# Moving the activations to 2048-byte boundaries, and loading the residual stream in two parts

## The chip, the core and the metric

The kernel runs on one core of a Trainium2 chip, as one program. The metric is the device time of an execution in microseconds (us), and the number that counts is the median of the runs. Five engines work on their own instruction streams and meet at semaphores: PE (TensorE, the matmuls), DVE (VectorE), ACT (ScalarE), POOL (GpSimd) and SP (SyncE, which here only issues DMAs). Data lives in SBUF (128 partitions, one flat byte address within each) and in PSUM, into which PE writes.

## The reference, cut to what matters

The input is one sequence of 512 tokens with 1024 features in float32. A state-space layer (S5) with a gated output and an MLP come first, then a layer of sliding-window attention and another MLP, then a last norm:

```python
h = x
h = h + s5_mixer(rmsnorm(h, norm_mix[0]), ...)          # 64 groups of 16 channels, 64 states each
#   inside: y = gelu(S5(u) + d * u);  z = y @ w_glu + b_glu;  return val * sigmoid(gate)
h = h + square(relu(rmsnorm(h, norm_mlp[0]) @ w_mlp_in[0])) @ w_mlp_out[0]
k, v = split(rmsnorm(h, norm_kv) @ w_kv + b_kv)
h = h + attention(rmsnorm(h, norm_mix[1]), k, v, sinks)  # window 128
h = h + square(relu(rmsnorm(h, norm_mlp[1]) @ w_mlp_in[1])) @ w_mlp_out[1]
return rmsnorm(h, norm_final)
```

## The kernel before, in words

**Layout.** Activations are held feature by token: a tile is 128 features by 512 tokens, 2048 bytes in each partition, and eight tiles make the 1024 features. `h` is the residual stream (8 tiles). `hid` and `act` hold operands of matmuls as pairs of float32r tensors, a high part (`[:, 0]`) and a low part (`[:, 1]`), so that three matmuls (high by high, high by low, low by high) give nearly float32 accuracy.

**Weight units.** Every dense layer is cut into units: one unit is a panel of 128 output features by all 1024 inputs (4096 bytes in each partition, 512 KB), 24 matmuls of 128 by 128 by 512. There are 164 units in a fixed order, numbered from the gated output of S5 (0 to 15: `U_GLU`) through the first MLP, K/V, Q, O and the second MLP. SP loads panel `u` into one of two buffers (`raw`), POOL splits it into `w_hi` and `w_lo` (the function `split`, which copies at L405 and subtracts at L408, in four slots), and PE multiplies (`unit`, L1114 to L1116; or `paired`, L1078 to L1080, which runs two units tile by tile). The semaphores between them are `raw_in` (a panel has landed), `w_split` (units split so far) and `unit_done` (units multiplied so far). PE waits at a unit's start for `w_split`; the first `paired` call takes units 0 and 1, the second (`paired(U_GLU + 2, ...)`) units 2 and 3. For K and V the operands change sides for one part (L1176 to L1178): there `act` is the stationary operand and the weights are what streams.

**Before the units.** S5 runs in eight steps of 8 groups ("octets"). PE's matmuls there are small and in plain float32; ACT evacuates their results, POOL and DVE do the complex arithmetic, and for each octet SP issues eight small DMAs (L298) that lay a small table `k_even` or `k_odd` out as a block Toeplitz matrix, `toep`. `y_mm` counts the octets that PE has finished. Units 0 and 1 are run in pieces between the last octets' work.

**SP's queue.** SP issues in program order: first the parameters, the input `xy`, the columns `col` and panels 0 and 1; then the 64 Toeplitz DMAs; then all of `h` (L305), panels 2 and 3 (L308), panels 4 to 7 (L311), the attention mask, and a loop over the rest. It cannot load `h` earlier in this version, because `w_2`, one of three buffers of S5 weights (octets 2 and 5), lies on the first 4608 bytes of `h`. ACT and DVE wait for `h` (`s_h`) before the gated output's epilogue (L531, L829, L833).

**Where things lie.** The tensors are allocated one behind the other, so each address follows from the sizes ahead of it. `h` starts at byte 16512 of a partition (8 x 2048 + 128), `w_hi` at 41088 and `w_lo` at 57472 (both 128 bytes above a multiple of 2048), and `hid` at 89184, which is 43 x 2048 + 1120; `act` and `qT`, which share one place behind it, are at 154720, again 1120 above a multiple.

Of the kernel before, what the change touches and what calls it, by code (L numbers as in the profile page):

```python
# [14 lines left out]
P = 128  # L15
D = 1024
L = 512
KT = D // P
# [66 lines left out]
SETUP_EXP, SETUP_PH, SETUP_L, SETUP_X, SETUP_MS = 4, 10, 23, 43, 47  # L85
SETUP_R8, SETUP_RSTD = 6, 10
T_DMA = 16 * J

STAT_A = (1, 3, 4, 5)

# [5 lines left out]
def build(nc, panels, xu_d, x_d, lam_d, prm_d, dd_d, cst_d, mask_d, col_d, out_d):  # L96
    ctx = ExitStack()
    with ctx:
        def sb(name, shape, dt=F32, where=ctx):
            return where.enter_context(nc.sbuf_tensor(name, shape, dt))  # L100

        def sem(name):
            return ctx.enter_context(nc.semaphore(name))


        before = ExitStack()
        w_2 = sb("w_2", [P, 2, OGP, J + 1, C], where=before)
        before.close()
        h = sb("h", [P, KT, L])
# [20 lines left out]
        t1 = sb("t1", [P, L])  # L130
        t2 = sb("t2", [P, 2, L])
        gate_sb = sb("gate_sb", [P, 2])
        phases = t1.rearrange("p (g k) -> p g k", k=NK)
        ph_round = rstd.rearrange("p (g k) -> p g k", k=NK)

# [71 lines left out]
        s_lam, s_prm, s_cst, s_h, s_col, s_mask, s_dd = (sem(n) for n in (  # L207
            "lam_in", "prm_in", "cst_in", "h_in", "col_in", "mask_in", "dd_in"))
# [31 lines left out]
        def wait(eng, s, value):  # L240

            if not (isinstance(value, int) and value <= 0):
                eng.wait_ge(s, value)
# [33 lines left out]
        @block.sync  # L277
        def _(sp):
            sp.dma_start(lam[:], lam_d).then_inc(s_lam, 16)
            sp.dma_start(prm[:], prm_d).then_inc(s_prm, 16)  # L280
            sp.dma_start(cst[:], cst_d).then_inc(s_cst, 16)
            sp.dma_start(dd[:], dd_d).then_inc(s_dd, 16)
            for c in range(4):
                part = slice(2 * c * OCT, (2 * c + 2) * OCT)
                sp.dma_start(xy[:, part, :], xu_d[:, part, :]).then_inc(s_xu[c], 16)
            sp.dma_start(col[:], col_d).then_inc(s_col, 16)
            for s in range(2):
                sp.dma_start(raw[:, s, :], panels[s]).then_inc(raw_in[s], 16)

            def toeplitz(o):  # L290

                q = o % 2
                wait(sp, k_evac, 4 * o + 4)
                wait(sp, zeroed, 3)
                wait(sp, y_mm, o - 1)
                for j in range(J):
                    r = J - 1 - j
                    sp.dma_start(toep[r * C:(r + 1) * C, q, :, :, j * C:],  # L298
                                 k_out[q][:, :, :, 0:(J - j) * C]).then_inc(t_in[q], 16)

            for o in range(NO):
                toeplitz(o)

            wait(sp, y_mm, NO - 2)
            sp.dma_start(h[:], x_d).then_inc(s_h, 16)  # L305
            for u in (2, 3):
                wait(sp, w_split, u - 1)
                sp.dma_start(raw[:, u % 2, :], panels[u]).then_inc(raw_in[u % 2], 16)  # L308
            for u in range(4, 8):
                wait(sp, w_split, u - 1)  # L310
                sp.dma_start(raw[:, u % 2, :], panels[u]).then_inc(raw_in[u % 2], 16)  # L311
            wait(sp, y_lo, KT)
            sp.dma_start(mask[:], mask_d).then_inc(s_mask, 16)
            with sp.Fori(4, NU // 2) as i:
                for s in range(2):
                    sp.wait_ge(w_split, 2 * i + s - 1)
                    sp.sem_inc(passed, 1)
                    sp.dma_start(raw[:, s, :], panels[2 * i + s]).then_inc(raw_in[s], 16)
            for m in range(KT):
                wait(sp, out_t, m + 1)  # L320
                sp.dma_start(out_d[m], h[:, m, :]).then_inc(out_s, 16)
            sp.wait_ge(out_s, 16 * KT)
# [100 lines left out]
        def _(a):  # L423
# [51 lines left out]
            def evacuate_k(o):  # L475
                wait(a, k_mm, o + 1)
                wait(a, t_in[o % 2], T_DMA * (o // 2))
                for x in range(4):
# [44 lines left out]
                wait(a, stat_v, 2 * n + 2)  # L523
                act_fn(rstd[:], stat[:], ACT.Sqrt).then_inc(stat_a, 1)

            wait(a, s_h, 16)
            wait(a, s_col, 16)
            with a.Fori(0, KT // 2) as i:
                for e in range(2):
# [69 lines left out]
        def _(v):  # L599
# [164 lines left out]
            def y_to_lo(o):  # L764
                wait(v, y_hi, o + 1)
                if o == NO - 2:
                    wait(v, t_in[1], T_DMA * NO // 2)
                tt(hid[:, 0, 1, o, :], ps[:, 7, :], hid[:, 0, 0, o, :].bitcast(F32), sub).then_inc(y_lo, 1)
# [50 lines left out]
                    nc.vector.reciprocal(scol[:], scol[:]).then_inc(stat_c, 1)  # L819


            wait(v, s_h, 16)
            wait(v, s_col, 16)
            with v.Fori(0, KT // 2) as i:
                for e in range(2):
# [162 lines left out]
        def _(pe):  # L988
# [51 lines left out]
            def outputs(o):  # L1040

                q = o % 2
                wait(pe, gelu_done, o)
                wait(pe, t_in[q], T_DMA * (o // 2 + 1))
                for g in range(OGP):
# [350 lines left out]
```

## Time and profile before

| | us |
|---|---|
| three runs | 1140.38, 1139.22, 1138.17 |
| median | 1139.22 |
| the profiled execution, its own time | 1139.55 |
| its span (first to last instruction) | 1137.7 |
| PE busy in the span | 1084.1 (95%) |
| PEld (weight loads, beside PE) busy | 879.7 (77%) |
| DVE, POOL, ACT busy | 640.1, 718.9, 202.7 |
| mean clock granted to PE | 0.98 of full |

PE is the engine that sets the time: it is busy in 95% of the span, and in the two MLPs in all of it. A matmul's record overlaps the next one's, so the rate of the matmuls is read from the distance between their starts, not from their durations. Idle time on the other engines costs nothing until PE waits for them.

### The profile page before, as it was taken

What the parts mean: (1) busy time and instruction counts of PE and PEld (TensorE: products, weight loads), DVE (VectorE), ACT (ScalarE), POOL (GpSimd) and SP (SyncE); (2) the same over time, 40 slices, a digit from 0 to 9 for tenths busy, and PEclk for the clock granted to TensorE, in tenths of its full rate; (3) what the DMA queues carried; (4) which work ended last, traced back from release to release, by engine and by line L of the source; (5) the groups of instructions that cost most, each with busy time, mean ns of one, the idle gap of its engine ahead of it and who ended that gap; (6) DMA issues with size and microseconds to landing.
All of it is one profiled execution on the core that took longest, in us unless ns stands there. A gap on an engine that the chain in (4) does not pass through costs nothing.

```text
span 1137.7 us, 16116 instructions
## 1 busy us (share of the span) xinstructions
PE 1084.1 (95%) x5720; PEld 879.7 (77%) x5720; DVE 640.1 (56%) x766; ACT 202.7 (18%) x439; POOL 718.9 (63%) x563
## 2 busy tenths in 40 slices
PE   4889999999999999999999999969999999999995
PEld 1778788788888888888788888757888888888884
DVE  7996574776316316417837876586762263164164
ACT  4763111111001001001105445111110010010000
POOL 7995977587667666667753220486766676676650
PEclk9799999999999999999999999989999999999998
DMA  4224332232222222222221110132223222222211
GB/s 184 33 33 134 130 111 92 74 111 92 93 92 93 92 93 93 99 98 89 90 81 62 38 38 1 38 111 66 101 92 98 93 99 99 93 92 93 92 56 74
DMA packets 34720, 97.91 MB, mean 86 GB/s; under 512 B 11120, under 2 KB 11504, under 8 KB 34416
## 3 DMA queue, kind: packets, MB, share of 16 engines
q1 hardware_dynamic: 34672, 97.24, 25.9%
q8 instruction: 34, 0.56, 0.2%
q14 instruction: 14, 0.11, 0.0%
HBM read 92.77 MB, written 2.10 MB: 83 GB/s over the span
## 4 chain that ended last, share of the span: by engine, by line
PE 84%; issue 4%; DVE 4%; ACT 3%; POOL 2%; DMA 2%; SPq 1%; DVEq 1%; ACTq 0%; POOLq 0%
PE ps L1114 23%; PE ps L1116 23%; PE ps L1115 23%; PE ps L1230 3%; PE ps L1207 2%; PE ps L1078 2%; PE ps L1079 2%; PE ps L1080 2%; PE ps L1219 1%; DVE act L803 1%; SPq L298 1%; DMA raw<-panels_in 1%; PE ps L1054 1%; PE ps L1016 1%; PE ps L1032 1%
## 5 line engine op out<-in xcount | busy, mean ns | idle before, releaser
L408 POOL TENSOR_TENSOR w_lo<-raw,w_hi 128x1024 fp32r<-128x1024 f32 x164 | 421.6, 2571 | 13.7
L1114 PE MATMUL ps<-hid,w_hi 128*128 128x512 f32 x736 | 294.7, 400 | 2.8 <-issue 1.9
L1116 PE MATMUL ps<-hid,w_lo 128*128 128x512 f32 x736 | 291.7, 396 | 0.0
L1115 PE MATMUL ps<-hid,w_hi 128*128 128x512 f32 x736 | 291.7, 396 | 0.0
L332 POOL TENSOR_TENSOR gate_sb<-gate_sb 128x1 f32<-128x1 f32 x164 | 42.5, 259 | 363.1 <-PE ps L1116 314.5
L1114 PE MATMUL ps<-act,w_hi 128*128 128x512 f32 x464 | 183.7, 396 | 1.2 <-DVE act L803 1.2
L1116 PE MATMUL ps<-act,w_lo 128*128 128x512 f32 x464 | 183.5, 396 | 0.0
L1115 PE MATMUL ps<-act,w_hi 128*128 128x512 f32 x464 | 183.5, 395 | 0.0
L405 POOL TENSOR_SCALAR w_hi<-raw 128x1024 fp32r<-128x1024 f32 x164 | 180.4, 1100 | 0.0
L862 DVE TENSOR_TENSOR h<-ps,h 128x512 f32 x64 | 44.2, 690 | 236.7 <-PE ps L1116 236.7
L1114 PEld LDWEIGHTS ps<-hid,w_hi 128*128 128x128 f32 x736 | 138.6, 188 | 36.9 <-issue 2.0
L1116 PEld LDWEIGHTS ps<-hid,w_lo 128*128 128x128 f32 x736 | 138.7, 188 | 33.6
L1115 PEld LDWEIGHTS ps<-hid,w_hi 128*128 128x128 f32 x736 | 138.7, 188 | 33.1
L851 DVE TENSOR_TENSOR hid<-t,hid 128x512 fp32r<-128x512 f32 x64 | 129.3, 2020 | 44.9 <-ACT hid L543 44.9
L543 ACT ACTIVATE hid<-t 128x512 fp32r<-128x512 f32 x64 | 40.7, 635 | 470.1 <-DVE t L849 470.1
L1114 PEld LDWEIGHTS ps<-act,w_hi 128*128 128x128 f32 x464 | 87.2, 188 | 22.6 <-DVE act L803 1.6
L1116 PEld LDWEIGHTS ps<-act,w_lo 128*128 128x128 f32 x464 | 87.2, 188 | 21.1
L1115 PEld LDWEIGHTS ps<-act,w_hi 128*128 128x128 f32 x464 | 87.2, 188 | 21.0
L847 DVE SCALAR_TENSOR_TENSOR t<-ps,rstd 128x512 f32<-128x512 f32 x64 | 44.2, 690 | 64.3 <-PE ps L1116 64.0
L849 DVE TENSOR_TENSOR t<-t 128x512 f32<-128x512 f32 x64 | 67.2, 1050 | 2.2
L800 DVE TENSOR_TENSOR acc<-acc,t 128x512 f32<-128x512 f32 x32 | 66.0, 2062 | 3.2
L517 ACT ACTIVATE act<-h,col x24 | 17.4, 725 | 143.2 <-DVEq L864 79.6
(209 smaller groups left out, 1084.3 us busy)
## 6 DMA issues: line engine op xcount, KB each, us to landing
raw<-panels_in SPq DMA_DIRECT2D x164, 512.0 KB, 3.2
xy<-xu_in SPq DMA_DIRECT2D x4, 512.0 KB, 7.8
h<-x_rows_in SPq DMA_DIRECT2D x1, 2048.0 KB, 9.0
out<-h SPq DMA_DIRECT2D x8, 256.0 KB, 2.1
prm<-prm_in SPq DMA_DIRECT2D x1, 1280.0 KB, 5.6
mask<-mask_in SPq DMA_DIRECT2D x1, 512.0 KB, 4.1
dd<-dd_in SPq DMA_DIRECT2D x1, 256.0 KB, 5.9
toep<-k_even SPq DMA_DIRECT2D x4, 64.0 KB, 2.3
```

Source lines behind the costliest of these rows:

```text
L332: nc.gpsimd.tensor_tensor(gate_sb[:, 0:1], gate_sb[:, 1:2], gate_sb[:, 1:2], ALU.mult)
L405: nc.gpsimd.tensor_scalar(w_hi[:, s, :], raw[:, s % 2, :], 1.0, 0.0, ALU.mult, ALU.add).then_inc(w_hi_done, 1)
L408: nc.gpsimd.tensor_tensor(w_lo[:, s, :], raw[:, s % 2, :], w_hi[:, s, :].bitcast(F32), ALU.subtract).then_inc(w_split, 1)
L543: act_fn(hid[:, par, 0, m, :], t2[:, m % 2, :], ACT.Copy).then_inc(hid_hi, 1)
L800: tt(acc[:], acc[:], t1[:], ALU.add).then_inc(sq_acc, 1)
L847: stt(t1[:], ps[:, m % 4, :], 0.0, rstd[:], ALU.max, ALU.mult).then_inc(bank_free, 1)
L849: tt(t2[:, m % 2, :], t1[:], t1[:], ALU.mult).then_inc(hid_sq, 1)
L851: tt(hid[:, par, 1, m, :], t2[:, m % 2, :], hid[:, par, 0, m, :].bitcast(F32), ALU.subtract).then_inc(hid_lo, 1)
L862: tt(tile(h, m), ps[:, s, :], tile(h, m), ALU.add).then_inc(bank_free, 1)
L1114: mm(ps[:, bank, :], w_hi[:, s, w], x[:, 0, k, :], start=(k == 0), stop=False)
L1115: mm(ps[:, bank, :], w_hi[:, s, w], x[:, 1, k, :], start=False, stop=False)
L1116: last = mm(ps[:, bank, :], w_lo[:, s, w], x[:, 0, k, :], start=False, stop=(k == KT - 1))
```

## The change

It has two parts. (1) Behind `gate_sb` a tensor of 232 float32 (928 bytes) that nobody uses is allocated, so that everything behind it lies 928 bytes higher: `hid` at 90112, which is 44 x 2048, and `act` at 155648, which is 76 x 2048. The S5 tensors and the Toeplitz tables move by the same 928 bytes; `h`, `raw`, `w_hi` and `w_lo` stay. (2) `h` is loaded by two DMAs. The first takes tiles 0 to 4 and is issued at the program's start behind panels 0 and 1; the second takes tiles 5 to 7 and is issued behind panels 2 and 3. `w_2` moves onto tiles 5 to 7 of `h`, clear of the first part. ACT and DVE wait for both parts.

```diff
@@ -85,6 +85,8 @@
+H_FIRST = KT - 3
+TO_LINE = 232
@@ -104,6 +106,7 @@
         before = ExitStack()
+        sb("h_first", [P, H_FIRST, L], where=before)
         w_2 = sb("w_2", [P, 2, OGP, J + 1, C], where=before)
         before.close()
         h = sb("h", [P, KT, L])
@@ -130,6 +133,7 @@
         gate_sb = sb("gate_sb", [P, 2])
+        sb("to_line", [P, TO_LINE])
@@ -286,6 +290,7 @@
             for s in range(2):
                 sp.dma_start(raw[:, s, :], panels[s]).then_inc(raw_in[s], 16)
+            sp.dma_start(h[:, 0:H_FIRST, :], x_d[:, 0:H_FIRST, :]).then_inc(s_h, 16)
@@ -302,10 +307,10 @@
             wait(sp, y_mm, NO - 2)
-            sp.dma_start(h[:], x_d).then_inc(s_h, 16)
             for u in (2, 3):
                 wait(sp, w_split, u - 1)
                 sp.dma_start(raw[:, u % 2, :], panels[u]).then_inc(raw_in[u % 2], 16)
+            sp.dma_start(h[:, H_FIRST:, :], x_d[:, H_FIRST:, :]).then_inc(s_h, 16)
             for u in range(4, 8):
@@ -523,7 +528,7 @@
-            wait(a, s_h, 16)
+            wait(a, s_h, 32)
@@ -819,7 +824,7 @@
-            wait(v, s_h, 16)
+            wait(v, s_h, 32)
```

The instruction streams of PE, DVE, ACT and POOL hold the same operations in the same order as before; only SP's changes. This is SP's stream before, from its last Toeplitz DMA of the last octet (`k_odd` is the table, `x_rows_in` the residual stream in memory, `panels_in` the weights; sizes are partitions by elements):

```order
L298 DMA toep<-k_odd 16x8x16
L305 DMA h<-x_rows_in 128x4096
L308 DMA raw<-panels_in 128x1024 x2
L311 DMA raw<-panels_in 128x1024 x4
L313 DMA mask<-mask_in 128x1024
```

And this is the same place after; panels 2 and 3 are now next to the Toeplitz DMA, and three eighths of `h` come behind them:

```order
L303 DMA toep<-k_odd 16x8x16
L312 DMA raw<-panels_in 128x1024 x2
L313 DMA h<-x_rows_in 128x1536
L316 DMA raw<-panels_in 128x1024 x4
L318 DMA mask<-mask_in 128x1024
```

The other five eighths are issued at the program's start. SP's first rows before:

```order
1 L279 DMA lam<-lam_in 128x233
2 L280 DMA prm<-prm_in 128x2560
3 L281 DMA cst<-cst_in 128x384
4 L282 DMA dd<-dd_in 128x512
5 L285 DMA xy<-xu_in 128x1024 x4
6 L286 DMA col<-col_in 128x346
7 L288 DMA raw<-panels_in 128x1024 x2
8 L298 DMA toep<-k_even 16x1024
```

And after, where one DMA stands between panels 0 and 1 and the first Toeplitz DMA:

```order
5 L289 DMA xy<-xu_in 128x1024 x4
6 L290 DMA col<-col_in 128x346
7 L292 DMA raw<-panels_in 128x1024 x2
8 L293 DMA h<-x_rows_in 128x2560
9 L303 DMA toep<-k_even 16x1024
```

So the whole of `h` moves in two pieces: 2560 elements of each partition ahead of S5, 1536 behind it.

## Rows read from the trace of the kernel before

**Rows 1.** Busy time of each engine, from the page.
```profile
PE 1084.1 (95%) x5720; PEld 879.7 (77%) x5720; DVE 640.1 (56%) x766; ACT 202.7 (18%) x439; POOL 718.9 (63%) x563
```

**Rows 2.** PE's waits: line waited for, us in total, times, longest.
```profile
PE ps L1078 <- DVE h L967: 9.4, 1, 9.4
PE ps L1078 <- POOL w_lo L408: 2.7, 1, 2.7
PE ps L1047 <- DMA toep<-k_even: 1.2, 1, 1.2
```

**Rows 3.** PE's timeline: start us, us, instruction [idle before <-releaser].
```profile
115.15 0.40 PE L1080 MATMUL ps<-hid,w_lo 128*128 128x512 f32 x1
118.21 0.50 PE L1078 MATMUL ps<-hid,w_hi 128*128 128x512 f32 x1 [2.65 <-POOL w_lo L408]
118.54 0.39 PE L1079 MATMUL ps<-hid,w_hi 128*128 128x512 f32 x1
...
196.47 0.40 PE L1116 MATMUL ps<-hid,w_lo 128*128 128x512 f32 x1
196.71 0.40 PE L1078 MATMUL ps<-act,w_hi 128*128 128x512 f32 x1
```

**Rows 4.** POOL's timeline, splits of units 2 to 5.
```profile
110.89 0.19 POOL L332 TENSOR_TENSOR gate_sb<-gate_sb 128x1 f32<-128x1 f32 x1 [13.55 <-DMA raw<-panels_in]
...
115.81 2.34 POOL L408 TENSOR_TENSOR w_lo<-raw,w_hi 128x1024 fp32r<-128x1024 f32 x1
118.11 0.19 POOL L332 TENSOR_TENSOR gate_sb<-gate_sb 128x1 f32<-128x1 f32 x1
...
124.96 2.70 POOL L408 TENSOR_TENSOR w_lo<-raw,w_hi 128x1024 fp32r<-128x1024 f32 x1
```

**Rows 5.** SP's timeline, DMA issues between 90 and 120 us.
```profile
94.91 5.50 SPq L298 DMA_DIRECT2D toep<-k_odd  x8
100.45 0.59 SPq L305 DMA_DIRECT2D h<-x_rows_in  x1
101.08 0.91 SPq L308 DMA_DIRECT2D raw<-panels_in  x2
114.60 13.42 SPq L311 DMA_DIRECT2D raw<-panels_in  x4
```

**Rows 6.** The page's DMA issues: KB each, median us from issue to landing.
```profile
raw<-panels_in SPq DMA_DIRECT2D x164, 512.0 KB, 3.2
h<-x_rows_in SPq DMA_DIRECT2D x1, 2048.0 KB, 9.0
```

**Rows 7.** Issue to landing at L308 (panels 2 and 3), then L288 (panels 0 and 1).
```profile
DMA to landing us min/median/max: 9.6/10.0/10.4
...
DMA to landing us min/median/max: 9.9/10.3/10.7
```

**Rows 8.** SP's timeline at the start: panels 0 and 1, first Toeplitz issues.
```profile
5.21 0.96 SPq L288 DMA_DIRECT2D raw<-panels_in  x2
33.56 5.98 SPq L298 DMA_DIRECT2D toep<-k_even  x8
```

**Rows 9.** DVE's timeline: last S5 state of L762, then the first epilogue.
```profile
101.87 0.41 DVE L762 TENSOR_TENSOR st<-ps,rs 128x256 f32<-128x256 f32 x1
117.81 0.75 DVE L829 SCALAR_TENSOR_TENSOR t<-ps,col,t 128x512 f32<-128x512 f32 x1 [3.98 <-ACT t L531]
118.71 1.72 DVE L833 TENSOR_TENSOR h<-t,h 128x512 f32 x1 [0.16 <-DVE t L829]
```

**Rows 10.** PE's timeline in the first MLP, matmuls 24 apart.
```profile
305.12 0.40 PE L1116 MATMUL ps<-hid,w_lo 128*128 128x512 f32 x1
...
310.72 0.40 PE L1116 MATMUL ps<-hid,w_lo 128*128 128x512 f32 x1
```

**Rows 11.** PE's timeline in K/V: the first, two in the middle, the last of 96.
```profile
570.35 0.28 PE L1176 MATMUL ps<-w_hi,act 128*128 128x256 f32 x1
...
571.40 0.28 PE L1176 MATMUL ps<-w_hi,act 128*128 128x256 f32 x1
...
571.75 0.28 PE L1176 MATMUL ps<-w_hi,act 128*128 128x256 f32 x1
...
581.43 0.27 PE L1178 MATMUL ps<-w_hi,act 128*128 128x256 f32 x1
```

**Rows 12.** PE's timeline, two matmuls behind its long wait.
```profile
763.12 0.63 PE L1079 MATMUL ps<-act,w_hi 128*128 128x512 f32 x1
763.55 0.63 PE L1080 MATMUL ps<-act,w_lo 128*128 128x512 f32 x1
```

**Rows 13.** Windows: us, busy of PE, PEld, DVE, ACT, POOL, PEclk, DMA share, GB/s.
```profile
100.00:200.00 100.00, 97.34 (x506) 77.71 (x505) 52.27 (x44) 17.52 (x22) 72.15 (x54) 1.00 0.36 127
760.00:765.00 5.00, 3.75 (x9) 2.97 (x10) 4.66 (x5) 2.01 (x2) 4.25 (x2) 0.50 0.35 105
1000.00:1100.00 100.00, 100.00 (x431) 80.49 (x430) 44.36 (x38) 4.45 (x7) 67.40 (x53) 1.00 0.27 92
```

**Rows 14.** The page's groups of matmuls in `unit`: count, busy, mean ns.
```profile
L1114 PE MATMUL ps<-hid,w_hi 128*128 128x512 f32 x736 | 294.7, 400 | 2.8 <-issue 1.9
L1114 PE MATMUL ps<-act,w_hi 128*128 128x512 f32 x464 | 183.7, 396 | 1.2 <-DVE act L803 1.2
```

## The prediction

> **What bounds the kernel now.** I began with the page's first part: PE is busy in 95% of the span [rows 1], so only what makes PE wait or changes its pace can move the end. Two questions follow: where does PE stand still, and at what pace does it run. The list of PE's waits answers the first. The reader should look there for waits that this change can reach: one, 2.7 us at L1078 on POOL's split (the second `paired` call, units 2 and 3) [rows 2]. The long one, 9.4 us on DVE at L967, is in front of the second MLP, and neither part of the change touches what leads to it. In the timeline the last matmul of units 0 and 1 starts at 115.15 us and the first of unit 2 at 118.21 [rows 3]. The window from 100 to 200 us has PE busy for 97.34 of 100 us [rows 13]: this wait is the whole loss there.
>
> Then I followed the wait back. POOL stood idle for 13.55 us until panel 2 landed, began at 110.89, and ended the second split at 115.81 + 2.34 = 118.15 us, which is what PE waited for [rows 4]. Panel 2 was issued at 101.08 [rows 5] and took 9.6 us to land, panel 3 took 10.4 [rows 7]; the median panel takes 3.2 us [rows 6]. The reason stands in the row ahead of it: the 2048 KB of `h` were issued at 100.45 [rows 5] and took 9.0 us [rows 6], so they landed at 109.5, then panel 2 at 110.7, and panel 3 (issued some 0.5 us behind it) at 111.9. They land in the order of issue, 1.2 us apart, as if in one queue: 512 KB in 1.2 us is the rate.
>
> **Part 2, the two loads of `h`.** *Removed:* the copy of 2048 KB in front of panels 2 and 3. The first of them takes its place at 100.45 us. The copy of `h` there needed 9.0 us, of which 4 x 1.2 = 4.8 us is transfer by the rate above, and 4.2 us is start-up (the last Toeplitz DMAs are still draining). Panel 2 then lands at 100.45 + 4.2 + 1.2 = 105.9 us at the latest, and with the median 3.2 us at 103.7 at the earliest. POOL is ready: besides the panel its third split waits only for octet 7's states, which DVE ends at 101.87 + 0.41 = 102.3 us [rows 9]. From panel 2's landing to the end of both splits it took 118.15 - 110.7 = 7.45 us. So the splits end between 111.1 and 113.3 us, and PE wants them at 115.38 (one matmul behind 115.15). The wait goes, with 2.1 us to spare in the worse case.
>
> *What it is worth.* From 115.15 to 118.21 are 3.06 us [rows 3]; without a wait a step takes 0.23 to 0.24 us, as where PE goes from one unit to the next at 196.47 and 196.71 [rows 3]. That is 2.82 us. The first matmul behind the wait is also slow to start the next one (0.33 us from 118.21 to 118.54, against 0.23), another 0.10. Sum: 2.9 us.
>
> *What is late next.* The second part of `h` (3/8 of it, 1.8 us of transfer) lands 1.2 + 1.8 us behind panel 2, at 106.7 to 108.9 us, and nobody needs it before L829 and L833 at 117.81 and 118.71 us [rows 9]; these follow PE's end of units 0 and 1, which does not move, so ACT and DVE wait for nothing new. Panel 4 was issued when POOL had split unit 2, at 114.60 [rows 5], and will be issued some 5 us earlier. Units 4 and 5 are wanted by PE from 115.38 + 2 x 5.6 = 126.6 us on (a unit is 5.60 us [rows 10]). Their splits need unit 1 and then unit 2 of PE: in the trace they took from 118.11 to 127.66 us [rows 4], 9.55 us for two with a wait of half a microsecond in between. Begun at 115.4 they end at 125.0; unit 4's is done by 120. The cover is 6 us for unit 4 and 7 for unit 5 (wanted at 132.2), and grows, since POOL needs about 4.5 us for a unit and PE 5.6. From there on PE's later waits are for DVE work that itself follows PE's last unit, so they move along with it; I count no part of the 2.9 us as given back.
>
> *Added:* one DMA of 5 of 8 tiles at the start. Panels 0 and 1 are issued from 5.21 to 6.17 us and land up to 10.7 us after [rows 7, 8], by 16.4. The new copy is behind them: 2.5 panels, 3.1 us, done by 19.5. The next DMA that SP issues is the Toeplitz one at 33.56 us [rows 8]. Cost nothing, covered by 14 us; SP's issue of 0.5 us falls into the same gap. If the queue did not serve in order but shared, the parameters would be up to 3.1 us late and the gain would be gone; the landings 1.2 us apart speak for order.
>
> **Part 1, the 928 bytes.** No operation is added; the question is whether an address changes a pace. PE's pace is the costly one: 3 x (736 + 464) matmuls of 512 columns in `unit` [rows 14] and 3 x 96 more in `paired` are 3888, so one nanosecond in each is 3.9 us. The row: 24 of them take 310.72 - 305.12 = 5.60 us, 233.3 ns each, at a granted clock of 1.00 (2.4 GHz) [rows 10, 13]. That is 560 cycles for 512 columns. At a clock of 0.50 (1.2 GHz) they start 0.43 us apart [rows 12, 13], 512 cycles: at the lower clock the 48 extra cycles are not there, so at the higher one something that feeds PE limits it. 20 ns x 3888 = 78 us is thus the most that an address could give back.
>
> Does it come from the address? K/V is the test that lies in the trace, for there the streamed operand is the weights, at 128 and not 1120 bytes above a multiple of 2048. 95 steps take 581.43 - 570.35 = 11.08 us [rows 11], 116.6 ns for 256 columns: 280 cycles, the same 35/32 per column. And its operand moves by 512 bytes with each k, so it runs over a multiple of 2048 only at k = 3 and k = 7; the three matmuls of k = 3 take 571.75 - 571.40 = 0.35 us, the same as the average of 3 x 116.6 = 0.35. So crossing a 2048-byte boundary costs nothing that is visible, and the offset of 1120 costs no more than that of 128. I take zero. Ends for the range: nothing excludes boundaries of 512 bytes or less. If each 512-byte boundary cost 12 of the 48 cycles (4 in an operand of 2048 bytes, 2 in K/V's two pieces of 512, which fits both rows), an aligned operand would have 3 inside instead of 4: 5 ns x 3888 = 19 us less. With 256-byte boundaries, 6 cycles each, it is 2.5 ns and 10 us less. On the other side the same 10 us more, if aligned operands met one boundary more.
>
> For the Toeplitz DMAs and S5's tensors, moved by the same 928 bytes, the bound is what PE waits for them: 1.2 us once [rows 2], a gain at most; a landing slower by as much would cost the same. Nearest to zero, which I take.
>
> The Trainium skill (page "TensorE: Matmul & The Clock Gate", section "Wait — 56ns, not 53.3ns?") has back-to-back matmuls at N / 2.4 GHz plus about 2.5 ns, 215.7 ns for 512 columns; this trace disagrees with 233.3 ns for float32r. By that rule 17.5 ns x 3888 = 68 us would be there to be won, if the address were what is in the way; the page doesn't say that it is. Against it stands a second rule: the page "SBUF — State Buffer" (section "Door 1: The DMA port swizzle", its note on cachelines) has lines of 16 bytes, and the old address 89184 is a multiple of 16 already, so by this rule the sum stays at 2.9 us.
>
> **The sum.** The profiled execution: 1139.55 - 2.9 = 1136.65 us. It was 0.33 above the median of 1139.22, so for a median I say **1136.4 us**, 0.25% less. A measurement of this kernel tells about 0.2% (2.3 us, below 1136.9) from no change, so the forecast lies just beyond it.
>
> **The rivals.**
> (a) *PE's pace rises.* One cause behind the 48 cycles (boundaries of 512 bytes or less) makes it 19 or 10 us less beside the 2.9: 1117 or 1127 us; the whole of it would be 1136.4 - 78 = 1058. For it: the extra cycles are real and feed-bound. Against it: K/V's same ratio at another offset, and no dependence on k. 10% together.
> (b) *The gain is given back.* The 2.9 us come back as a wait later: either the early copy delays the parameters (3.1 us), or PE's clock falls for longer somewhere, since behind its 9.4 us wait it is at 0.50 [rows 2, 13] and a shift of 3 us may lengthen that stretch. 1138.5 to 1139.5 us. 16%.
> (c) *Slower.* At the new address a streamed operand of 2048 bytes costs one stop more than it does now, in all 3888 matmuls; it decides from 1.3 ns each on ((2.9 + 2.3) / 3888). With the 2.5 ns of above: 1136.4 + 9.7 = 1146 us. For it only that one nanosecond is so dear; against it the same K/V rows. 5%.
> (d) *The change doesn't do what it says*: panels 2 and 3 stay late since what delays them is the start-up of 4.2 us and not `h`. Even twice that start-up ends the splits at 117.55 instead of 118.15, 0.6 us won: 1138.6. The landings 1.2 us behind `h` speak against it. 3%.
>
> **How the numbers follow.** Forecast 66%, (a) 10, (b) 16, (c) 5, (d) 3. The forecast's own spread is the 1.2 us of the Toeplitz term and about 1 us by which runs differ (1138.17 to 1140.38): 1135.0 to 1137.6. The range of 8 in 10 takes in (b) and (d) and leaves out (a) and (c): 1134.6 to 1139.8. Faster: four fifths of the forecast's 66% lie beyond 0.2%, with (a) 0.63; within 0.2%: the rest of it, (b) and (d), 0.32; slower 0.05.
>
> **What would show it.** Step by step in the profile after: no wait of the second `paired` call on POOL's split, and 0.23 us between the starts where now are 3.06; panel 2 landing between 103.7 and 105.9 us and POOL's idle before it down to 6 to 8 us; both parts of `h` landed by 19.5 and 109; the first Toeplitz issue still near 33.6. PE's 24 matmuls in 5.60 us and K/V's 96 in 11.1 as before: any other number there makes part 1 real and my forecast wrong, the more so as one nanosecond is 3.9 us. A new wait of PE behind 118 us, or a longer stretch at a clock of 0.50, would be rival (b).

## The result, and the profile after

The changed kernel took 1133.03 us in the median (five runs, 1132.36 to 1134.47) against 1139.22: the ratio is 0.9947, with a 95% interval of 0.9933 to 0.9962. That is 6.2 us less. The forecast was 1136.4 with a range from 1134.6 to 1139.8: the direction was right, and the gain more than twice what was forecast (6.2 us against 2.8). The profiled execution took 1132.71 us, its span 1130.9.

The page's first part answers to [rows 1]. PE is busy 7.3 us less, with the same 5720 matmuls:

```profile
PE 1076.8 (95%) x5720; PEld 878.0 (78%) x5720; DVE 637.5 (56%) x766; ACT 202.4 (18%) x439; POOL 719.6 (64%) x563
```

PE's waits answer to [rows 2] (line waited for, us in total, times, longest). The wait of the second `paired` call for POOL's split is gone; the long one is still there, and the one for the first Toeplitz DMAs (L1052 now) has grown by 2.0. It costs nothing: PE's work ahead of it was done earlier (more of it at full clock), while the DMAs landed when they did before, and PE goes on at 40.81 us (40.83 before):

```profile
PE ps L1083 <- DVE h L972: 9.5, 1, 9.5
...
PE ps L1052 <- DMA toep<-k_even: 3.2, 1, 3.2
```

PE's timeline where units 0 and 1 end answers to [rows 3]: the next matmul starts 0.23 us behind the last.

```profile
114.47 0.39 PE L1085 MATMUL ps<-hid,w_lo 128*128 128x512 f32 x1
114.70 0.40 PE L1083 MATMUL ps<-hid,w_hi 128*128 128x512 f32 x1
```

POOL's timeline answers to [rows 4]. Its idle time ahead of the split of unit 2 has fallen from 13.55 to 6.35 us, and both splits end at 110.9, 3.8 us ahead of PE:

```profile
103.62 0.19 POOL L337 TENSOR_TENSOR gate_sb<-gate_sb 128x1 f32<-128x1 f32 x1 [6.35 <-DMA raw<-panels_in]
...
108.51 2.39 POOL L413 TENSOR_TENSOR w_lo<-raw,w_hi 128x1024 fp32r<-128x1024 f32 x1
```

SP's timeline answers to [rows 5] and [rows 8]: the early part of `h` at 6.34 us, the first Toeplitz DMA at 33.87 (33.56 before), then panels 2 and 3 and the late part.

```profile
6.34 0.49 SPq L293 DMA_DIRECT2D h<-x_rows_in  x1
33.87 5.69 SPq L303 DMA_DIRECT2D toep<-k_even  x8
...
99.63 1.00 SPq L312 DMA_DIRECT2D raw<-panels_in  x2
100.67 0.43 SPq L313 DMA_DIRECT2D h<-x_rows_in  x1
```

Their time from issue to landing, for L312 (panels), L293 (early part) and L313 (late part); the first answers to [rows 7]:

```profile
DMA to landing us min/median/max: 3.8/4.2/4.5
...
DMA to landing us min/median/max: 13.0/13.0/13.0
...
DMA to landing us min/median/max: 7.2/7.2/7.2
```

So panel 2 landed at 103.4 us, `h` at 19.3 and 107.9. All of that is as predicted, but for 0.3 us at panel 2. (One size was off without effect: the late part of `h` landed 3.3 us behind panel 3, where the prediction counted 1.8 us for it.) What was not predicted stands in PE's timeline in the first MLP, which answers to [rows 10]: the two matmuls 24 apart are 5.57 us apart and not 5.60.

```profile
299.74 0.39 PE L1121 MATMUL ps<-hid,w_lo 128*128 128x512 f32 x1
...
305.31 0.39 PE L1121 MATMUL ps<-hid,w_lo 128*128 128x512 f32 x1
```

Over longer stretches 24 matmuls take 5.600 us in the gated output and 5.577 in both MLPs. K/V went the other way; its first and last matmul (see [rows 11]) give 11.39 us for 95 steps, 119.9 ns each instead of 116.6:

```profile
565.38 0.28 PE L1181 MATMUL ps<-w_hi,act 128*128 128x256 f32 x1
...
576.77 0.29 PE L1183 MATMUL ps<-w_hi,act 128*128 128x256 f32 x1
```

This table sets the two profiled executions side by side. Each entry is a start in PE's timeline; the last column is what each stretch contributed.

| PE's start of | before | after | shift so far | contributed |
|---|---|---|---|---|
| last matmul of units 0, 1 | 115.15 | 114.47 | -0.68 | S5 and PE's clock in it: -0.7 |
| first of unit 2 | 118.21 | 114.70 | -3.51 | the wait: -2.8 |
| first of MLP 0 | 196.71 | 193.10 | -3.61 | -0.1 |
| last of MLP 0 | 555.72 | 550.70 | -5.02 | the pace: -1.4 |
| first of Q | 583.57 | 578.92 | -4.65 | K/V's pace and a longer wait ahead of it: +0.4 |
| last of O | 751.49 | 744.96 | -6.53 | PE's clock behind K/V: -1.6; the rest: -0.3 |
| last of MLP 1 | 1122.11 | 1114.48 | -7.63 | the pace: -1.4; wait and half clock ahead of it: +0.3 |
| end of the span | 1137.74 | 1130.93 | -6.81 | PE's clock in the tail: +0.8 |

The clock term can be seen in windows (us, busy of PE, PEld, DVE, ACT, POOL, granted clock, DMA share, GB/s). This one is of the kernel before, just behind its K/V wait: 10 matmuls at 0.50, which is 1.2 GHz.

```profile
584.20:587.60 3.40, 3.40 (x10) 2.62 (x9) 0.51 (x1) 0.00 (x0) 3.32 (x4) 0.50 0.27 93
```

And this one of the changed kernel at the same place: 16 matmuls at 1.00, 2.4 GHz.

```profile
579.20:582.60 3.40, 3.40 (x16) 2.76 (x15) 0.86 (x1) 0.00 (x0) 3.32 (x4) 1.00 0.16 35
```

### The profile page after: what moved, and what is told of

Read it like the earlier page. It is cut to its first block, busy times and chain, and to the rows that moved or that the text cites. A ratio compares the mean times of both kernels' runs of the same rounds, so it can differ in the third digit from the quotient of the medians.

```text
span 1130.9 us, 16118 instructions
## 1 busy us (share of the span) xinstructions
PE 1076.8 (95%) x5720; PEld 878.0 (78%) x5720; DVE 637.5 (56%) x766; ACT 202.4 (18%) x439; POOL 719.6 (64%) x563
## 4 chain that ended last, share of the span: by engine, by line
PE 83%; DVE 8%; issue 5%; ACT 2%; POOL 1%; DVEq 1%; DMA 0%; ACTq 0%; SPq 0%
PE ps L1119 23%; PE ps L1120 23%; PE ps L1121 23%; PE ps L1235 3%; PE ps L1083 2%; PE ps L1085 2%; PE ps L1084 2%; PE ps L1212 2%; PE ps L1224 1%; DVE act L808 1%; DVE h L867 1%; ACT s_sb L578 1%; ACT hid L522 1%; DVE t L802 0%; DMA prm<-prm_in 0%
## 5 line engine op out<-in xcount | busy, mean ns | idle before, releaser
L413 POOL TENSOR_TENSOR w_lo<-raw,w_hi 128x1024 fp32r<-128x1024 f32 x164 | 420.5, 2564 | 13.7
```

The costliest lines, as they stand in the source:

```text
L413: nc.gpsimd.tensor_tensor(w_lo[:, s, :], raw[:, s % 2, :], w_hi[:, s, :].bitcast(F32), ALU.subtract).then_inc(w_split, 1)
```

## The experiments

A time given without a number of runs is that of a single run. S5 takes unequal time from run to run: over all the profiles PE's last matmul of units 0 and 1 starts between 114.3 us (`before_again`) and 118.3 us (`dist_0`), after 7 to 27 us at half clock in S5. So a single run proves little by its total time; its paces, read from the trace, are what counts.

"Distance" below is the address of `hid` less that of `w_hi`, modulo 256 bytes; that of `act` and of `w_lo` is the same. It is 224 in the kernel before and 128 in the changed one.

**Each part alone, and both kernels again.** `split_only` is the changed kernel without the 928 bytes, `shift_only` the kernel before with them.

```diff
-        sb("to_line", [P, TO_LINE])          # split_only, against the changed kernel
+        sb("to_line", [P, 232])              # shift_only, against the kernel before
```

> Part 2 alone: h in two loads, hid still 1120 bytes above a multiple of 2048. Theory A (the two parts act apart: the loads remove PE's wait at units 2 and 3, the addresses set PE's pace): about 2.9 us under before, near 1136.3; 24 matmuls take 5.600 us everywhere as in before, K/V 116.7 ns a step. Theory B (the pace came by chance or with the time at which PE begins, not with the address): the pace of the first MLP drops to about 5.578 us for 24 here too, and the time is near 1133.5.

Measured: 1134.28 us median (8 runs), ratio 0.9963 (0.9951 to 0.9976); 5.600 us for 24 and 116.7 ns in K/V everywhere. The pace did not come with the loads, but the time is 2 us lower than theory A had it: 5.3 us under the kernel before beside it by the medians, 4.2 by the ratio. In its profile PE is at full clock behind K/V:

```profile
577.00:583.00 6.00, 4.14 (x24) 3.42 (x23) 2.57 (x5) 0.00 (x0) 4.63 (x5) 1.00 0.00 0
```

> Part 1 alone: 928 bytes, h in one load. Theory A: PE's wait of 2.7 us at units 2 and 3 is back, 24 matmuls in the two MLPs take 5.577 us, K/V 120 ns a step, and the time is some 2.5 us under before (3888 matmuls, of which those of the MLPs, 3072, gain 0.95 ns: 2.9, less 0.3 in K/V), near 1136.6. Theory B: the pace is 5.600 us for 24 and the time that of before.

Measured: 1136.69 us (11 runs), ratio 0.9975 (0.9966 to 0.9984), with the wait for POOL back (2.3 us idle, 2.7 from one start to the next), 5.577 us for 24 and 119.9 ns in K/V: near theory A's 1136.6. In this profile the half clock came behind the wait for unit 2, at 119.1 us, and not behind K/V:

```profile
119.10:122.50 3.40, 3.40 (x8) 2.75 (x9) 3.21 (x3) 0.72 (x1) 3.32 (x3) 0.50 0.45 154
```

> The changed kernel a second time. If PE's pace follows from the addresses, the same pattern returns: 5.600 us for 24 in the gated output, 5.577 in both MLPs, 120 ns in K/V. If it depends on the moment at which the stream begins, the stretches can take other values, for instance 5.600 in an MLP. The 3.4 us at half clock behind K/V (in the profile of before at 584 us, not in that of after) may come or not.

Measured: 1136.01 us. 24 matmuls took 5.577 us in the gated output and 5.600 in both MLPs, the reverse of the first profile, K/V 118.7 ns, and the half clock came behind K/V, at 580.7 us. So the same program at the same addresses runs at either of two paces. The slower one is not the kernel before's: its steps alternate between 229 and 238 ns, those of the kernel before between 232 and 235.

> The kernel before a second time. Address: 5.600 us for 24 matmuls in every stretch, 116.7 ns in K/V. Moment: some stretch at 5.577. The half clock at 584 us for 3.4 us comes again if it follows from the kernel's own activity, and may be missing if it is chance; without it the time is some 1.2 us less.

Measured: 1138.39 us, 5.600 us for 24 in every stretch, K/V 116.7, the half clock at 583.4 us again.

**The clock behind the waits.** The added matmuls are these; `before_fill` has both places, `split_fill` (on `split_only`) the second alone:

```diff
+            def fill(n):
+                for _ in range(n):
+                    mm(ps[:, 7, 0:256], ident, cst[:, 0:256], start=True, stop=True)
+            wait(pe, y_lo, KT)
+            fill(6)
             paired(U_GLU + 2, 2, hid[:, 0], (y_lo, 1))
...
+            wait(pe, bank_free, 4 + U_KV + 2)
+            fill(4)
             query_unit(0, range(KT))
```

> The kernel before (h in one load, old addresses) with matmuls added that nobody reads, where PE waits: 6 of 0.43 us in front of units 2 and 3 and 4 behind K/V, so that PE is busy there. Theory A (the 2 us by which splitting the loads won more than the wait itself are stretches of 3.4 us at half clock that follow from the waits at units 2/3 and behind K/V; each costs 1.5 to 1.7 us): the half clock behind units 1 and behind K/V is gone, and the time falls by 1.3 to 1.7 us under before, to about 1138.0, with a narrow spread. Rival B (the clock has nothing to do with it): the time stays at 1139.5 and single runs spread as before.

Measured: 1137.49 us median of 12 runs, 2.0 under the 1139.51 of the kernel before beside it; but four of the twelve are above 1138.9, and the ratio of 0.999 (0.9981 to 0.9998) says 1.1 us. In the profile both places are at full clock; behind unit 1:

```profile
117.40:120.80 3.40, 3.40 (x16) 2.72 (x16) 3.21 (x3) 0.71 (x1) 3.14 (x3) 1.00 0.42 154
```

> h in two loads at the old addresses, with the 4 added matmuls behind K/V. Theory A: the half clock behind K/V can no longer come, the time is that of the two-load kernel in its usual runs (1134.2) or up to 0.5 above it, since the added matmuls can end a little late, and about 3 us under before_fill, which is the wait of 2.8 us alone. Rival B: the difference to before_fill stays at 5 us.

Measured: 1134.69 us (1134.19 to 1135.05), 2.8 us under `before_fill`: with the clock held up, the two loads are worth about what the wait was, as predicted (by the two ratios it is 3.4 us, with some 2 us of uncertainty). It is 0.4 us above `split_only`, so in the kernel with two loads the added matmuls won nothing. Theory A holds, though the size of the clock's share is known only as 1 to 2 us.

**Whose address sets the pace.** `all_shift` puts the 928 bytes in front of `h`, so that weights and activations move together; `both_at_0` puts 1920 bytes there and 1056 behind `gate_sb`.

```diff
+        sb("pad", [P, 232])                  # all_shift, no to_line;  both_at_0: 480, TO_LINE = 264
         before = ExitStack()
```

> 928 bytes put in front of h instead of behind gate_sb, h in two loads: hid and act are on multiples of 2048 as in the changed kernel, and the weights move along (w_hi and w_lo from 128 to 1056 above a multiple), so that the distance between the two operands is that of before. If the streamed operand's own address sets the pace: steps alternate by 229 and 238 ns or run in the seven-step pattern, 5.577 or 5.600 us for 24, and K/V takes 118.6 to 119.9 ns. If the distance between the two operands that PE reads at once sets it: steps of 232 and 235, 5.600 everywhere, K/V 116.7.

Measured: 1134.27 us, and exactly the numbers of the kernel before: steps of 232 and 235 ns, 5.600 us for 24, K/V 116.7. `hid` is on a multiple of 2048 here, and nothing is won by it. Two matmuls 24 apart:

```profile
300.26 0.40 PE L1120 MATMUL ps<-hid,w_lo 128*128 128x512 f32 x1
...
305.86 0.40 PE L1120 MATMUL ps<-hid,w_lo 128*128 128x512 f32 x1
```

The distance counts, not `hid`'s own address.

> h, raw, w_hi, w_lo, hid and act all on multiples of 2048 (the weights now too), h in two loads. Own address: as in the changed kernel, 5.577 or 5.600, K/V 118.6 to 119.9. Distance between the operands: a value not seen yet, since the distance is new (0); if both reads want the same line at once it could be slower than 5.600.

Measured: 1118.56 us. The guess that it might be slower was wrong by a wide margin: 24 matmuls take 5.440 us, 226.7 ns each.

**The distance, step by step.** Only `TO_LINE` differs from the changed kernel:

```diff
-TO_LINE = 232
+TO_LINE = 264      # dist_0;   392: dist_512;   328: dist_256;   280: dist_64;   320: dist_224
```

> The changed kernel with 1056 unused bytes in place of 928: hid and act 128 bytes above a multiple of 2048, as w_hi and w_lo are, so that the distance between the two operands that PE reads at once is 0 modulo 2048, while neither is on a multiple. Distance theory: the pace of both_at_0, 5.440 us for 24 matmuls, K/V 120 ns, and a time near 1119. Own-address theory (a multiple of 2048 of each operand is what counts): 5.577 to 5.600, as in the kernel before or the changed one, near 1133 to 1136.

Measured: 1117.39 us median of 5, ratio 0.9798 (0.978 to 0.9817), 5.440 us for 24, though neither operand is on a multiple of 2048. The timeline of its first MLP, two matmuls 24 apart:

```profile
300.10 0.39 PE L1121 MATMUL ps<-hid,w_lo 128*128 128x512 f32 x1
...
305.54 0.39 PE L1121 MATMUL ps<-hid,w_lo 128*128 128x512 f32 x1
```

> 1568 unused bytes: hid and act 640 above a multiple of 2048, a distance of 512 from the weights. The 8 weight slices of a unit already lie 512 bytes apart and all take the same time, so if the distance theory holds the pace is the same as at distance 0, 5.440 us. Only if 2048 itself is the period is it another value.

Measured: 1113.9 us in one run, 5.440.

> 1312 unused bytes: hid and act 384 above a multiple of 2048, a distance of 256 from the weights. Period of 256 bytes or less: 5.440 us as at distance 0. Period of 512: another value, between 5.44 and 5.60.

Measured: 1115.61 us in one run, 5.440. So the period is 256 or less.

> 1184 unused bytes: hid and act 192 above a multiple of 2048, a distance of 64 from the weights. Period of 64 or less: 5.440 us, but then the changed kernel (distance 128) would show it too, so I expect another value: 5.577 to 5.600, or one between.

Measured: 1124.84 us (the unused bytes are 280 x 4 = 1120, not 1184; the distance is 64 as stated), a third value, 5.493 us for 24, in steps of 226, 229 and 232 ns. Its timeline, 24 apart:

```profile
300.21 0.39 PE L1121 MATMUL ps<-hid,w_lo 128*128 128x512 f32 x1
...
305.70 0.39 PE L1121 MATMUL ps<-hid,w_lo 128*128 128x512 f32 x1
```

> The changed kernel with 1280 unused bytes: hid and act 352 above a multiple of 2048, 224 above the weights. In the kernel before they are 992 above them, and 992 is 3 x 256 + 224. If the distance counts modulo 256: exactly the numbers of before, 5.600 us for 24 in steps of 232 and 235 ns, K/V 116.7. If another modulus or the address itself counts, another value.

Measured: 1136.85 us, 5.600 us for 24 and 116.7 ns in K/V, as said. `hid` is 352 bytes above a multiple of 2048 here and 1120 in the kernel before; what they share is the distance modulo 256.

| distance modulo 256 | kernels | us for 24 matmuls of 512 columns | ns a step in K/V |
|---|---|---|---|
| 0 | both_at_0, dist_0, dist_256, dist_512, dist_0_one_load | 5.440 | 119.9 |
| 64 | dist_64 | 5.493 | 113.5 |
| 128 | the changed kernel (3 profiles), shift_only | 5.577 or 5.600 | 118.7 to 119.9 |
| 224 | before (2 profiles), split_only, all_shift, dist_224, both fills | 5.600 | 116.7 |

One rival remains to the distance between PE's two operands. All that lies behind `gate_sb` moves together, so the distance between `hid` and what other engines read or write ahead of it changes too. The traces speak against it: in the first MLP (290 to 540 us) of the kernel before, PE's steps that overlap work of POOL take 233.3 ns in the mean and those that don't 233.4; in `dist_0` it is 226.7 and 226.6, and DVE, ACT and the DMAs make no more difference.

**What was still open.**

> The changed kernel a third time: at a distance of 128 the pace has so far been 5.577 in both MLPs (twice, one of it with h in one load) and 5.600 (once). Two-pace theory: again exactly one of the two in each stretch, and K/V 119.9 or 118.7. A value between them would speak against it.

Measured: 1134.0 us, 5.577 in the gated output, both MLPs and O, 5.600 in Q, K/V 119.9, and the half clock behind K/V at 580.1. No value lies between the two, and one execution can change from one to the other.

`dist_0_one_load` is `shift_only` with 264 in place of 232.

> The kernel before with 1056 unused bytes: distance 0, h in one load. If the two parts act apart: 5.440 us for 24 matmuls, PE's wait for units 2 and 3 back at 2.5 to 3 us, and 3 to 5 us over dist_0, 1120.5 to 1122.5 (the wait of 2.8 and, in some runs, the half clock behind it).

Measured: 1119.96 us median of 4 (1114.56 to 1120.79), 2.6 us over `dist_0`, with the wait back (2.3 us idle, 2.7 from start to start) and 5.440 us for 24. Against the kernel before the ratio is 0.9816 (0.979 to 0.9842). The two parts add up within what these runs can tell; the time is half a microsecond under what was expected.

`dist_0_fill` is `dist_0` with `fill(4)` behind K/V and `fill(21)` in front of the second MLP.

> dist_0 with matmuls added that nobody reads, 4 behind K/V and 21 in front of the second MLP, where PE waits 10 us. In dist_0 PE runs at half clock for 3.4 us behind K/V in some runs (1.6 us lost) and for 10 to 14 us around the start of the second MLP, 4 to 6 of them with matmuls of the MLP (2 to 3 us lost). If activity alone keeps the clock up, both go: 2 to 4 us under dist_0, near 1114. If not, 1117 or, where the added matmuls end late, above.

Measured: 1112.19 us (1110.77 to 1113.44), ratio 0.9762 (0.9747 to 0.9777): 5.2 us under `dist_0` by the medians, 4.1 by the ratios, so at or above the upper end of what was expected, and 27 us under the kernel before. It beats both kernels. The windows at the start of the second MLP show why; first `dist_0`, 14 matmuls at half clock:

```profile
749.10:754.90 5.80, 5.75 (x14) 4.51 (x15) 4.02 (x3) 2.00 (x2) 3.06 (x2) 0.50 0.41 144
```

and `dist_0_fill`, 25 at full clock:

```profile
743.80:749.60 5.80, 5.76 (x25) 4.80 (x26) 4.04 (x3) 2.01 (x2) 3.07 (x2) 1.00 0.38 142
```

## Why the prediction was right or wrong

**Right: part 2.** The copy of `h` in front of panels 2 and 3 was what made PE wait. Panel 2 landed at 103.4 us (said: 103.7 to 105.9), both splits ended at 110.9 (111.1 to 113.3), the step was 0.23 us, and the wait of 2.8 us went; with PE's clock held up the medians of the kernels with one load and with two differ by the same 2.8 us (`before_fill`, `split_fill`). To the hundredth that is luck: the step that the wait lengthens is 2.5 to 3.1 us in the four profiles with one load and no added matmuls. The early part of `h` cost nothing, DMAs landed in order, and no later wait took the place of the one removed. Rival (d) falls.

**Wrong: "I take zero" for part 1.** The step that failed is the test by K/V. It was read as "the streamed operand lies at another offset there (128, not 1120), and the pace per column is the same 35/32, so the address does not matter". But in K/V the two operands change roles: the weights stream and `act` is loaded as the stationary one. Both are the same tensors at the same addresses, so the distance between them is the same in size, 32 bytes off a multiple of 256 on one side or the other. The test varied the streamed operand's own address, which doesn't count, and not the size of the distance, which does. That it gave 35/32 twice was taken as a law per column and is an accident of that distance: at the changed kernel's distance the units get faster and K/V slower, at distance 0 the units take 0.443 ns a column and K/V 0.468, and at distance 64 K/V is the fastest of all (113.5 ns).

The bounds built on it had the wrong cause as well. "Boundaries of 512 or 256 bytes" inside one operand gave 10 or 19 us for any aligned `hid`; `all_shift` has an aligned `hid` and wins nothing. What the address could give back was put at 78 us at most; the best that was found is 5.600 - 5.440 = 0.16 us for 24, or 6.7 ns in each of 3888 matmuls, 26 us by that count. The medians say 17 us (`dist_0` against `split_only`) and 19 us (`dist_0_one_load` against the kernel before). Part of the difference is that PE then waits longer for DVE: behind the first MLP 2.3 us instead of 1.1, and in front of the second MLP 10.0 instead of 9.4. In the changed kernel itself the gain is 0.96 ns for each of the MLPs' 3072 matmuls, 2.9 us, less 0.3 in K/V, and only in runs that fall into the faster of its two paces; three of four profiles at that distance did in their MLPs. `shift_only` measured 0.9975, 2.8 us. On top of the two loads it is less: the changed kernel lies 1.3 us under `split_only` by the medians, 1.8 by the ratios.

**Mis-sized: the wait's worth in the kernel before.** The sum had 2.9 us for part 2; `split_only` measured 5.3 by the medians and 4.2 by the ratio. So of the 3.3 us by which the sum fell short, about as much lies here as in part 1: 2.4 us against 1.3 by the medians, 1.3 against 1.8 by the ratios. The sum priced the wait at what PE lost while it stood still. It costs more, because PE's clock is at 0.50 for 3.4 us behind it in some runs. In each of the four profiles of kernels with one load and no added matmuls, the half clock came at exactly one of two places: behind unit 1 (at 119.1 and at 118.6 us) or behind K/V (584.2 and 583.4); it costs 1.5 to 1.7 us. With two loads there is one place for it instead of two, and 4 of 11 profiles without added matmuls have it at neither. (Three profiles at distances 0 and 64 have another stretch at 0.50 ahead of K/V, which begins between 550 and 553 us.) Adding matmuls at both places won 1.1 us by the ratio, 2.0 by the medians. That rival (b) counted the clock only as a way to lose the gain was one-sided: the prediction looked at the 9.4 us wait, where it fell before as after, and not at the two short ones.

**The rest.** Rival (a) was nearest in kind (PE's pace rises with the address) but for the wrong reason, and its 1117 us was met by `dist_0`, not by this change. Rival (c), one stop more in each matmul, did not come for the units; only K/V got slower, by 3.2 ns a matmul. How the 6.2 us split in the median is only known roughly: 2.8 the wait, 0 to 2.5 the pace, 1 to 2 the clock.

**Left open.** Why the distance of the two operands sets the pace, why K/V goes by another order of distances than the units, and what decides between 5.577 and 5.600 at distance 128, no run here shows. Distances other than 0, 64, 128 and 224 were not tried, so that 256 is the period is shown for 0 (three distances) and 224 (two).

## What to carry to other kernels

Where PE is the bound and streams float32r, take the distance between the start addresses of the stationary and the streamed operand modulo 256 into account, and try 0 first: 1056 unused bytes alone gave 1.8% here (`dist_0_one_load`). An operation in which two operands only change places is no test of an address effect, since it keeps the size of their distance. And a short wait of PE costs more than its length where the clock falls behind it; matmuls that nobody reads can hold it up.

## What the runs showed of the hardware that was not expected

- PE's pace for 128x128x512 float32r matmuls depends on where its two operands lie relative to each other: 226.7 ns each at distance 0, 228.9 at 64, 232.4 or 233.3 at 128, 233.3 at 224, always at a granted clock of 1.00. The Trainium skill (page "TensorE: Matmul & The Clock Gate", section "Step-by-step: what each phase is for") says that loading the next tile's weights doesn't take read bandwidth from the running matmul; here `hid` is on a multiple of 2048 in `both_at_0` as in the changed kernel, the distance to the weights differs (0 instead of 128), and the pace is 226.7 ns instead of 232.4 or 233.3. That speaks against the sentence for float32r; which of PE's reads waits for which, no row shows.
- No distance tried came down to the 215.7 ns that the same page, in the section "Wait — 56ns, not 53.3ns?", has for 512 columns; the nearest is 226.7.
- At one and the same distance (128) the pace can take two values, 5.577 or 5.600 us for 24 matmuls, from run to run and between stretches of one execution, and stays with one of them for hundreds of microseconds.
- A wait of PE of about 2 us can be followed by 3.4 us at a granted clock of 0.50: behind 2.3 us of idle time at unit 2 in `shift_only`, behind 1.9 us at the end of K/V in the kernel before. It did not come every time.
- Twenty-one added matmuls (9 us) in front of the second MLP kept the clock at 1.00, where without them it was at 0.50 for 13.7 us in the profile of `dist_0` (from 741.2 us); this and the four behind K/V were worth 5.2 us in the medians, 4.1 by the ratios.
